# First token tiles of a decoder block: the second tile squared earlier on ScalarE, and the second half of the first weight slab rounded ahead of the first tile's second half

## The reference

```
h = RMSNorm(x) * norm_mix                      # x: 512 x 1024
proj = h @ w_in                                # w_in: 1024 x 4648, sliced into q, k, v, index and gate parts
o_sb = stick_breaking(...); o_sa = sparse_attention(...)
y = (sigmoid(g_sb) * (o_sb @ W_sb) + sigmoid(g_sa) * (o_sa @ W_sa)) @ W_out
x = x + y
x = x + relu(RMSNorm(x) @ W1)^2 @ W2
```

## Time and profile before

| what | value |
|---|---|
| median of 3 executions | 716.02 us (715.8, 716.02, 716.7) |
| profiled execution | 716.59 us, of which the span from first to last instruction 714.9 us |
| PE busy | 708.0 us, 99% of the span |
| DVE busy | 556.3 us, 78% |
| ACT busy | 349.8 us, 49% |
| POOL busy | 225.8 us, 32% |
| chain that ended last, by engine | PE 97%, DVE 1%, ACT 1% |

### The profile page before, as it was taken

One profiled execution on the slowest core, in us unless ns is written; L12 is line 12 of the kernel. 1 busy time (PEld: TensorE's weight loads), 2 busy tenths in 40 slices (PEclk: granted clock), 3 DMA queues, 4 the chain that ended last, 5 costly groups with the idle time before them and its releaser, 6 DMA issues.

```text
span 714.9 us, 9720 instructions
## 1 busy us (share of the span) xinstructions
PE 708.0 (99%) x3430; PEld 570.8 (80%) x3430; DVE 556.3 (78%) x801; ACT 349.8 (49%) x498; POOL 225.8 (32%) x184
## 2 busy tenths in 40 slices
PE   8999999999999999999999999999999999999997
PEld 5878878787777777788889888888888888888886
DVE  7354888999885885569986688795959778695897
ACT  6245653365666877832644452536244361534441
POOL 2104324002230000010131280907245270806586
PEclk9999999999999999999999999999999999999999
DMA  9308332312110212289353215051422406031103
GB/s 334 145 16 243 111 93 84 118 47 72 60 60 1 62 57 60 78 228 235 136 177 119 99 52 175 30 176 59 159 76 96 139 0 198 37 117 60 60 0 118
DMA packets 46150, 74.84 MB, mean 105 GB/s; under 512 B 2721, under 2 KB 27553, under 8 KB 46114
## 3 DMA queue, kind: packets, MB, share of 16 engines
q1 hardware_dynamic: 44528, 71.21, 30.2%
q0 software_dynamic: 1584, 3.15, 2.5%
q10 hardware_dynamic: 2, 0.00, 0.0%
HBM read 69.90 MB, written 2.10 MB: 101 GB/s over the span
## 4 chain that ended last, share of the span: by engine, by line
PE 97%; DVE 1%; ACT 1%; issue 0%; DMA 0%; ACTq 0%; DVEq 0%
PE ps L2148 8%; PE ps L2150 8%; PE ps L2149 8%; PE ps L2177 7%; PE ps L2179 7%; PE ps L2178 7%; PE ps L488 6%; PE ps L490 6%; PE ps L489 6%; PE ps L495 5%; PE ps L497 4%; PE ps L496 4%; PE ps L2132 2%; PE ps L2131 2%; PE ps L2133 2%; PE ps L2061 2%
## 5 line engine op out<-in xcount | busy, mean ns | idle before, releaser
L735 POOL TENSOR_TENSOR a_lo<-qo_sb,a_hi 128x512 fp32r<-128x512 f32 x56 | 94.1, 1705 | 35.3 <-ACT a_hi L1094 35.3
L2148 PE MATMUL ps<-b_hi,cut_hi 128*128 128x512 f32 (+1 forms) x280 | 104.0, 371 | 0.0
L2149 PE MATMUL ps<-b_lo,cut_hi 128*128 128x512 f32 (+1 forms) x280 | 103.8, 371 | 0.0
L2150 PE MATMUL ps<-b_hi,cut_lo 128*128 128x512 f32 (+1 forms) x280 | 103.8, 371 | 0.0
L1083 ACT ACTIVATE qo_sb<-ps 128x512 f32<-128x512 f32 x32 | 19.2, 599 | 127.1 <-PE ps L2150 81.0
L495 PE MATMUL ps<-cut_hi,a_hi 128*128 128x512 f32 x152 | 61.3, 403 | 0.0
L2150 PEld LDWEIGHTS ps<-b_hi,cut_lo 128*128 128x128 f32 x280 | 52.7, 188 | 9.1
L2149 PEld LDWEIGHTS ps<-b_lo,cut_hi 128*128 128x128 f32 x280 | 52.8, 188 | 9.0
L2148 PEld LDWEIGHTS ps<-b_hi,cut_hi 128*128 128x128 f32 x280 | 52.7, 188 | 9.0
L497 PE MATMUL ps<-cut_hi,a_lo 128*128 128x512 f32 x152 | 59.5, 392 | 0.0
L496 PE MATMUL ps<-cut_lo,a_hi 128*128 128x512 f32 x152 | 59.4, 391 | 0.0
(11 more groups left out here) (263 smaller groups left out, 1725.1 us busy)
## 6 DMA issues: line engine op xcount, KB each, us to landing
raw<-in_w_ff_dram SPq DMA_DIRECT2D x32, 1024.0 KB, 5.5
raw<-in_w_in_dram SPq DMA_DIRECT2D x16, 1024.0 KB, 5.9
gates<-in_x_dram SPq DMA_DIRECT2D x8, 512.0 KB, 5.3
raw<-in_w_out_dram SPq DMA_DIRECT2D x4, 1024.0 KB, 6.3
raw<-in_w_in_dram SPq DMA_DIRECT2D x4, 512.0 KB, 6.4
raw<-in_w_branch_sb_dram SPq DMA_DIRECT2D x2, 1024.0 KB, 5.0
raw<-in_w_branch_sa_dram SPq DMA_DIRECT2D x4, 512.0 KB, 6.3
qT_sa<-in_w_out_dram POOLq DMA_DIRECT2D x2, 1024.0 KB, 9.8
```

Of the source, the lines that this page charges most:

```text
L735: return pool.tensor_tensor(left_lo[:, q], left[q], left_hi[:, q].bitcast(F32), ALU.subtract).then_inc(l_lo, 1)
L2148: T.matmul(dst, w_hi[:, w], b_hi[:, k, a:b], start=(k == 0), stop=False)
L2149: T.matmul(dst, w_hi[:, w], b_lo[:, k, a:b], start=False, stop=False)
L2150: mm = T.matmul(dst, w_lo[:, w], b_hi[:, k, a:b], start=False, stop=(k == KD - 1))
```

## The change

On ACT the square of token tile 1 goes ahead of `norm_hi(0)`, and the rounding of slab 0's second half, with its wait for the load, goes ahead of `norm_hi(1)`. On DVE `norm_lo(1)` moves behind `norm_scale(1)` and `dve_cut(0, 1, 2)`. On PE a loop of four with a wait inside is written as two loops of two with the wait between them.

```
                     act_half(0)
-                    norm_hi(0, a_hi)
                 elif m == 1:
                     norm_square(1, x_tok[:, 1, :], slot(SQ, 2))
-                    norm_hi(1, a_hi)
+                    norm_hi(0, a_hi)
                     act.wait_ge(raw_in[0], 16)
                     act_cut(0, 1, 2)
+                    norm_hi(1, a_hi)
                     act_half(1)
...
             norm_lo(0, a_hi, a_lo)
-            norm_lo(1, a_hi, a_lo)
             norm_scale(1, x_tok[:, 1, :], x_tok[:, 1, :], mix_gain)
             dve_cut(0, 1, 2)
+            norm_lo(1, a_hi, a_lo)
             dve_half(1)
...
-                for k in range(4):
-                    if k == 2:
-                        pe.wait_ge(hi_done, 2)
+                for k in range(2):
+                    part(1, k, a_hi, cut_hi)
+                    part(1, k, a_lo, cut_hi)
+                pe.wait_ge(hi_done, 2)
+                for k in (2, 3):
                     part(1, k, a_hi, cut_hi)
                     part(1, k, a_lo, cut_hi)
```

## The result

The changed kernel takes 717.63 us (median of 13 executions, 716.26 to 718.5) against 715.80 us before (13 executions, 715.47 to 716.77). The ratio is 1.0022, 95% interval 1.0015 to 1.0029: 1.83 us slower, outside the range of 715.0 to 717.3 us that was forecast. The profiled execution took 717.62 us, its span is 715.9 us.

What follows compares the result with a forecast made beforehand. PE was taken as the bound, busy 708.0 of 714.9 us, early on held by its slow clock. The parts summed to 0.00 us, leaving the execution at 716.59 us; forecast the median, 716.0 us, range 715.0 to 717.3.

Steps and rivals of the forecast that it cites:

- the square of tile 1 ahead of `norm_hi(0)`: On ACT: starts at about 6.85 us in idle time, `norm_hi(0)` still starts at 8.12, 0.24 us to spare.
- The bound of 7.07 us: Latest landing of tile 1's load that leaves `norm_hi(0)` on time: 6.83 plus 0.24 us to spare.
- Rival (a): At PE's first product: tile 1 lands late and delays `norm_hi(0)`; 0 to 5.3 us, 1.8 taken, 717.8 us; chance 0.07.
- The end of 8.2 us: Latest landing assumed for tile 1's load, when the next transfer lands; price there 1.1 us.
- any delay of `norm_hi(0)` is a delay of PE, one for one: At PE's first product, 8.86 us, behind `norm_hi(0)` ending at 8.72: each delay costs PE its own length.
- The sum of the other parts: First tile on PE: worth 0.00 to 0.49 us by the moment of the clock's rise; 0.00 taken.
- the two waits that the sum gave for an early rise: PE in the old kernel, rise at 9.5 us or before: 0.24 to 0.44 us for `hi_done` 1, 0.26 for `lo_done` 1.
- PE's steps: PE in the first tile takes its steps at the same times: 0.00 us.
- ACT's and DVE's paces: Start-to-start times used for the new order: ACT 0.48 to 0.95 us, DVE 0.61 to 1.18 us.
- the loop that is written otherwise: On PE: same matmuls with the same waits in the same places, 0.00 us.
- POOL and SP: POOL's two small instructions move into idle time; SP's loads can be issued 0.9 to 1.5 us sooner; worth nothing.
- `nt_cut` 2: Semaphore for PE's second four transposes: raised at 12.37 instead of 10.97 us, needed at about 13.8, so harmless.

Runs made afterwards that it cites:

- the fixed delay: Kernel before with three more ACT squares that nobody reads ahead of `norm_hi(0)`: 718.07 us against 715.78, ratio 1.0036.
- the break filled: Changed kernel with three filler matmuls on PE between the first transposes and the first product: 716.00 us against 715.78, ratio 1.0001.
- the second look at before: Kernel before, run once more unchanged: 715.97 us, one execution.
- without the load: Changed kernel's order, but the square reads a slab half already there instead of tile 1, so the output is wrong: 715.46 us, ratio 0.9995.
- the wait alone: Kernel before with ACT waiting for tile 1's load ahead of `norm_hi(0)`, the square still behind it: 715.89 us, ratio 1.0000.
- all but the square: Changed kernel with `norm_hi(0)` ahead of the square of tile 1 again: 716.53 us, ratio 1.0009.

## Why the prediction was wrong

*The step that failed* is the first one, the square of tile 1 ahead of `norm_hi(0)`: "lands 5.1 us later, at 6.83 ... with 0.24 us to spare". In the profile after, the load landed 1.1 us later, the square's 1.03 us were not over when the first transposed half was there, and PE stood still for 1.06 us where the prediction had nothing. I took the landing of one execution for the kernel's. In the 13 profiles of this study (both kernels, all variants) the same transfer, issued at the same moment, landed 5.1 to 6.4 us behind its issue, 6.0 in the median; 5.1 is the smallest of all. The bound of 7.07 us is met by two of the 13. The traffic shows it: from 4.5 to 8.5 us the transfers ran at 400 GB/s in the profile before and at 324 in the one after (the last column, laid out as in the earlier trace rows), with the same loads queued. Over the 13 profiles the four landings of up to 5.5 us go with 381 to 406 GB/s in that stretch, the nine of 5.9 us or more with 321 to 372.

```profile
4.50:8.50 4.00, 3.62 (x10) 1.64 (x10) 2.89 (x5) 1.95 (x4) 0.75 (x2) 1.00 1.03 400
```

```profile
4.50:8.50 4.00, 3.85 (x11) 1.67 (x9) 2.80 (x5) 1.86 (x4) 0.75 (x2) 1.00 0.96 324
```

The kernel before could not show that, because nothing waited for the landing: the square stood behind `norm_hi(0)`, and a load at 8.0 us would have changed no row of PE, ACT or DVE. What sets the rate of the transfers in one execution is open. The Trainium skill (DMA: Bandwidth & Descriptors, "Queues, rings and completion order") says that completions are not first in, first out for an issuing engine; here the loads of lines 536 and 540 landed in the order of their issue in all 13 profiles, and it was the rate that moved.

*Rival (a)* was the right mechanism, with a chance of 0.07 that should have been the largest. That its price of 1.8 us is so near the 1.83 measured is luck: it was a third of a span from 0 to 5.3 us, and nothing was worked out for the third. The end of 8.2 us that I set to the landing came from the same one execution; in the profile after, that next transfer landed at 9.3. The question that I left out was by how much a landing scatters, with 0.24 us of cover.

*The price.* That "any delay of `norm_hi(0)` is a delay of PE, one for one" failed as well: the fixed delay of 1.26 to 1.52 us cost 2.29, and with the break filled a delay cost nothing that could be told. Rival (a) named both parts: the late first product, and a later rise of the clock. The experiments bear both out, but not how the 1.83 us divide between them. Where PE had no break between the transposes and the products, the rise was seen between 9.6 us (the second look at before) and 12.4; with a break of 0.5 to 1.3 us it was seen at 13.4 to 14.5, in four profiles. A longer break did not mean a later rise: 1.06 us went with 13.4, 0.54 us with 14.2. And 13.4 is not far from 12.4 for four profiles against nine; the weight lies on the medians of the fixed delay and of the filled break. The filled break gives the time back. That activity releases the clock and that the moment is not tied to the kernel's start is what the Trainium skill says (TensorE: Matmul & The Clock Gate, "What's actually happening"); these runs agree, since in one and the same kernel, the one before, the rise was seen at 9.6 and at 12.4 us.

*The sum of the other parts*, 0.00 to 0.49 us gained, was right as far as it can be told: without the load, the new order took 715.46 us against 715.86, a difference of 0.40 that the interval does not separate from none. The second look at before shows the two waits that the sum gave for an early rise: the product at 10.98 comes 0.20 us and the one at 13.08 0.27 us behind PE's pace, each just behind its semaphore (`act_cut(0, 1, 2)` done at 10.93, `dve_cut(0, 1, 2)` at 13.03). Without the load, the same steps of the new order follow at pace (10.69 to 10.94 and 12.06 to 12.85), and its tile takes 7.44 us for 7.83. That is one execution of each. I took 0.00 because the earlier trace rows show the rise at 12.4. Of the nine profiles without a break only one more shows it as late (the wait alone); the other seven show it between 9.6 and 11.8. How often the kernel before itself has the late rise is not shown by its two profiles.

*PE's steps, ACT's and DVE's paces, the loop that is written otherwise, POOL and SP*: right. With the square on time DVE's rows came within 0.1 us of the times worked out (`norm_lo(1)` at 11.62 for 11.68). ACT's two roundings of second halves came later, again because of their loads (9.28 for 8.62 and 11.97 for 11.00), and PE did not need them sooner.

*`nt_cut` 2.* I held that the later `norm_lo(1)` is harmless. It is so only with tile 1's root early; all but the square shows 1.05 us of wait for it.

## What to carry to other kernels

A single profile gave an instruction's duration well and a transfer's landing badly (over the profiles of this study `norm_hi(0)` took 0.57 to 0.60 us wherever it has a row of its own, the load 5.1 to 6.4): before work is moved in front of the critical engine's next input, ask how far the load that this work waits for scatters, and treat a cover smaller than that as none. A step that only waited for a load behind the critical work tells nothing about how late the load may come, since nobody was there to wait. And while TensorE was at its lower level, a delay that left it idle cost more than its length (2.29 us for at most 1.52); fillers in the break were cheaper than the break (716.00 us against 717.63).

## What was not expected of the hardware

One transfer of 512 KB, issued at 1.7 us in every run, landed between 5.1 and 6.4 us later, in a program whose whole time, in the kernel before, repeats within 0.2% (715.47 to 716.77 us). The column of the granted clock stood at 1.00 in the very stretches in which matmuls of 512 columns were 0.43 us apart, so at the start of this kernel the level had to be read from the starts.
